# First FFN of a two-block transformer kernel: vectors loaded from ScalarE's queue, constants behind the weights, the context's second half turned ahead of the down products

## The reference, cut to what matters

```python
def swiglu(x, w_gate, w_up, w_down):
    return (jax.nn.silu(x @ w_gate) * (x @ w_up)) @ w_down
# first stage of first_block:  x = layer_norm(ALPHA * x + 0.5 * swiglu(x, gate, up, down), g, b)
```

## Time and profile before

| | us |
|---|---|
| median of 3 runs | 2466.32 (2464.76 to 2466.33) |
| profiled execution | 2465.18 |
| its span (first to last instruction) | 2462.6 |
| PE busy | 2277.5 (92% of the span) |
| DVE busy | 1439.2 (58%) |
| ACT busy | 1129.9 (46%) |
| mean granted TensorE clock | 0.964 of 2.4 GHz |
| DMA, mean over the span | 141 GB/s |

### The profile page before, as it was taken

The page is one execution under the profiler, slowest core; times in us unless marked ns, Lnnn a source line. Parts: engine busy times, 40 slices in busy tenths (PEclk is TensorE's granted clock), DMA queues, the critical chain, the costliest instruction groups (busy, mean ns, idle before and its releaser), DMA issues. The chain is left out here.

```text
span 2462.6 us, 37937 instructions
## 1 busy us (share of the span) xinstructions
PE 2277.5 (92%) x14504; PEld 1882.8 (76%) x14504; DVE 1439.2 (58%) x2366; ACT 1129.9 (46%) x1918; POOL 80.2 (3%) x117
## 2 busy tenths in 40 slices
PE   6999989999999989999769997889999989998998
PEld 6787967888888877877447886668888778876886
DVE  6565257667665347665554666364545554446886
ACT  3344254444443345444266665343434444445554
POOL 0000000000000000000001222000000000000000
PEclk9999999999999999999899999889999988998999
DMA  8786334875887414873112120144343353304662
GB/s 240 235 268 211 63 120 151 268 258 155 252 265 231 110 69 145 261 250 112 53 42 74 49 70 2 35 120 125 105 126 106 112 144 86 94 2 146 196 190 92
DMA packets 389938, 346.83 MB, mean 141 GB/s; under 512 B 24388, under 2 KB 353464, under 8 KB 389304
## 3 DMA queue, kind: packets, MB, share of 16 engines
q1 hardware_dynamic: 380600, 294.80, 40.6%
q10 hardware_dynamic: 9216, 50.34, 5.2%
HBM read 344.05 MB, written 1.05 MB: 140 GB/s over the span
## 5 line engine op out<-in xcount | busy, mean ns | idle before, releaser
L693 PE MATMUL ps<-x_hi_lo,gu_hi 128*128 128x512 f32 x1680 | 423.7, 394 | 1.9 <-DVE gu_sum L878 1.9
L693 PEld LDWEIGHTS ps<-x_hi_lo,gu_hi 128*128 128x128 f32 x1680 | 305.6, 188 | 80.9 <-issue 18.7
L878 DVE TENSOR_REDUCE gu_sum<-ps 128x256 f32<-128x512 f32 x220 | 150.6, 689 | 251.0 <-PE ps L695 248.8
L781 ACT ACTIVATE gu_hi<-w_gu 128x1024 fp32r<-128x1024 f32 x220 | 229.6, 1054 | 128.2 <-DVE gu_sum L878 52.8
L861 DVE TENSOR_TENSOR gu_lo<-w_gu,gu_hi 128x1024 fp32r<-128x1024 f32 x220 | 260.7, 1219 | 23.1 <-ACT gu_hi L781 22.9
L695 PEld LDWEIGHTS ps<-x_hi_lo,gu_lo 128*128 128x128 f32 x1680 | 228.8, 190 | 16.8
L695 PE MATMUL ps<-x_hi_lo,gu_lo 128*128 128x256 f32 x1680 | 233.8, 282 | 0.0
L722 PE MATMUL ps<-dn_hi,h_hi 128*128 128x512 f32 x440 | 174.2, 396 | 13.7 <-DVE h_lo L903 13.7
L722 PE MATMUL ps<-dn_lo,h_hi 128*128 128x512 f32 x440 | 173.2, 394 | 0.0
L722 PE MATMUL ps<-dn_hi,h_lo 128*128 128x512 f32 x440 | 171.9, 391 | 0.0
L797 ACT ACTIVATE silu<-gu_sum 128x256 f32<-128x256 f32 x88 | 36.7, 417 | 265.0 <-DVE gu_sum L878 264.4
(11 more groups left out here) (464 smaller groups left out, 4794.8 us busy)
## 6 DMA issues: line engine op xcount, KB each, us to landing
w_gu<-in_ffn_w_up SPq DMA_DIRECT2D x176, 512.0 KB, 6.3
w_dn<-in_ffn_w_down SPq DMA_DIRECT2D x132, 512.0 KB, 3.5
w_mod<-in_w_mod ACTq DMA_DIRECT2D x64, 768.0 KB, 7.0
w_gu<-in_ffn_w_gate SPq DMA_DIRECT2D x88, 512.0 KB, 5.1
odd_w<-in_odd_w_qkv SPq DMA_DIRECT2D x24, 512.0 KB, 5.2
w_gu<-in_ffn_w_down SPq DMA_DIRECT2D x11, 1024.0 KB, 4.9
hgrn_w<-in_even_w_in SPq DMA_DIRECT2D x20, 512.0 KB, 3.9
wo<-in_w_out SPq DMA_DIRECT2D x2, 4096.0 KB, 13.2
```

The source lines that it names most:

```text
L693: pe.matmul(gu(a), gu_hi[n][:, a, f, :], x_both[:, f, :, :], start=(f == 0), stop=False, skip_group_check=True)
L781: act.activation(gu_hi[n][:, a, :, :], wgu[n][:, a, :, :], ACT.Copy).then_inc(s["w_hi"], 1)
L878: dve.reduce_sum(c[n][:, a, :], gu(a).rearrange("p h t -> p t h"), AX.X).then_inc(s["c_ready"], 1)
```

## The change

The 15 vector loads leave SP's `load_rest` and become `load_vectors`, which ACT issues first of all, behind a one-column activation that reads a cleared cell. SP keeps constants and taps in `load_rest`. The context's two loads become `load_context`. The first pair of loads of the loop is written out for the first FFN: SP issues tile 2's gate and up part, its down part (when `dn_split` 1 has come), then the context, then tile 3; the loop starts one pair later. In step 3, `turn_rest` moves ahead of `down(2)` on TensorE, and `keep_rest` moves on DVE from the end of the step to right behind the reductions. Steps 1 and 2 keep the old order. Other FFNs of the program have no `Begin` and keep their code.

```diff
--- before.py
+++ after.py
@@ -478,6 +478,7 @@
         self.rows = ctx.enter_context(nc.sbuf_tensor("par_rows", [P, PAR_TILES, P], F32))
         self.x_rows = ctx.enter_context(nc.sbuf_tensor("x_rows", [P, TT, D], F32))
         self.causal = ctx.enter_context(nc.sbuf_tensor("causal", [P, P], F32))
+        self.warm = ctx.enter_context(nc.sbuf_tensor("warm", [P, 1], F32))
         self.consts = [(self.causal[:, :], w["c_causal"]), (k.cmp_mask[:, :, :], w["c_cmp"]),
                        (k.any_cmp[:, :], w["c_any"]), (k.unit[:, :], w["c_unit"]), (k.pick[:, :], w["c_stack"])]
 
@@ -487,18 +488,26 @@
             sp.dma_start(self.x_rows[:, tt, :], self.w["x"][0, tt * P:(tt + 1) * P, :]).then_inc(s["x_in"], 16)
         sp.dma_start(self.k.alpha[:, :], self.w["c_alpha"]).then_inc(s["alpha_in"], 16)
 
+    def load_vectors(self, act, s):
+        w, rows = self.w, self.rows
+        act.wait_ge(s["rows_zeroed"], 1)
+        act.activation(self.warm[96:P, :], rows[96:P, 2, 0:1], ACT.Copy)
+        for name, tile, r in self.VECTORS:
+            a = w[name]
+            src = a.rearrange("(r p) -> r p", p=P) if len(a.shape) == 1 else a.rearrange("l (r p) -> (l r) p", p=P)
+            act.dma_start(rows[r:r + src.shape[0], tile, :], src).then_inc(s["rows_in"], 16)
+
     def load_rest(self, sp, s):
         w, rows = self.w, self.rows
         for dst, src in self.consts:
             sp.dma_start(dst, src).then_inc(s["const_in"], 16)
         sp.wait_ge(s["rows_zeroed"], 1)
-        for name, tile, r in self.VECTORS:
-            a = w[name]
-            src = a.rearrange("(r p) -> r p", p=P) if len(a.shape) == 1 else a.rearrange("l (r p) -> (l r) p", p=P)
-            sp.dma_start(rows[r:r + src.shape[0], tile, :], src).then_inc(s["rows_in"], 16)
         taps = w["ffn_conv_w_2"].rearrange("l j (r p) -> (l j r) p", p=P)
         for n in range(CONV):
             sp.dma_start(rows[0:88, 2 + n, :], taps[88 * n:88 * n + 88, :]).then_inc(s["rows_in"], 16)
+
+    def load_context(self, sp, s):
+        w = self.w
         sp.wait_ge(s["x_turned"], FT // 2)
         for tt in range(TT):
             sp.dma_start(self.x_rows[:, tt, :], w["ctx_2"][0, tt * P:(tt + 1) * P, :]).then_inc(s["ctx_in"], 16)
@@ -670,9 +679,17 @@
                     else:
                         load_gu(n, n)
                         load_dn(n, n)
+                ahead_of_loop = 1 if begin else 0
                 if begin:
                     begin.load_rest(sp, s)
-                with sp.Fori(0, NF // 2 - 1) as j:
+                for n in range(2 * ahead_of_loop):
+                    sp.wait_ge(s["gu_split"], n + 1)
+                    load_gu(n + 2, n)
+                    sp.wait_ge(s["dn_split"], n + 1)
+                    load_dn(n + 2, n)
+                    if n == 0:
+                        begin.load_context(sp, s)
+                with sp.Fori(ahead_of_loop, NF // 2 - 1) as j:
                     for n in range(2):
                         sp.wait_ge(s["gu_split"], j * 2 + n + 1)
                         load_gu(j * 2 + (n + 2), n)
@@ -751,9 +768,11 @@
                         gate_up(t, n)
                     if mod and fixed == NF - 3:
                         mod_to_columns()
+                    if begin and fixed == 3:
+                        begin.turn_rest(pe, s, fixed)
                     if fixed is None or fixed >= 1:
                         down(t - 1, 1 - n, first=(fixed == 1 and not ln))
-                    if begin and fixed is not None:
+                    if begin and fixed is not None and fixed < 3:
                         begin.turn_rest(pe, s, fixed)
 
                 if begin:
@@ -774,6 +793,9 @@
 
             @block.scalar
             def _(act):
+                if begin:
+                    begin.load_vectors(act, s)
+
                 def hi_gu(t, n, a, fixed):
                     if a == 0:
 
@@ -878,6 +900,8 @@
                         dve.reduce_sum(c[n][:, a, :], gu(a).rearrange("p h t -> p t h"), AX.X).then_inc(s["c_ready"], 1)
                     if fixed == 0:
                         lo_dn(0, 5)
+                    if begin and fixed == 3:
+                        begin.keep_rest(dve, s, fixed)
                     if conv is not None:
                         dve.wait_ge(s["c_ready"], t * 2 + 2)
                         dve.wait_ge(s["mid_ready"], t * 2 + 2)
```

## The result

The changed kernel takes 2451.43 us (median of 4, 2450.14 to 2451.77) beside 2466.32 (median of 4): 14.9 us less, ratio of all runs 0.9936 with a 95% interval of 0.9921 to 0.9950. The predicted 2454.7 is 3.3 us above the measured median. That median lies at the lower end of the range of 2451.2 to 2461.2; by the ratio, 0.9936 times 2466.32 is 2450.5, just under it. The profiled execution took 2451.77, its span 2449.1, so between the two profiled executions the difference is 13.4 us, in span 13.5.

A forecast was written before the change was run, and what follows sets the result against it. TensorE bounds the kernel, with holes only before 64.8 us. Terms -12.1 first hole and clock, +0.2, +1.3, +0.1, +1.8, -2.8 second hole save 11.6 us: 2453.6, plus 1.14 to the median gives 2454.7 (2451.2 to 2461.2).

The forecast's parts named there:

- the two new waits of the sum: TensorE's predicted new waits: +1.3 us ahead of `down(1)` and +1.8 us ahead of the second context transposes.
- What bounds the kernel, and that savings before 64.8 us carry over: TensorE never idles in FFN steps from 64.8 to 204 us, so time saved earlier is saved for the whole program.
- Start, +0.2 (0 to 0.8): At the start, ACT's 15 issues fit its slack until 12.3 us; vector transfers delay the tokens by 0.2 us.
- First hole, -11.9: Ahead of `down(0)`: tile 2 issued earlier removes 9.9 us of hole and 2.2 of slow clock; `gate_up(2)` starts at 30.0.
- New wait ahead of `down(1)`, +1.3: Tile 3 lands at 33.0, `h_lo` ends at 36.9, TensorE is ready at 35.7: +1.3 us (0 to 3).
- Parameter copies, +0.1: After `down(1)`, DVE makes the parameter copies at about 39.8; no more than 0.1 us of wait.
- Second context transposes, +1.8: Behind `gate_up(3)`, TensorE waits for DVE's late context copies, done at 48.2: +1.8 us (0 to 2.5).
- Second hole, -2.8: Ahead of `mod_turn`: with the second half turned early, the 2.78 us wait for the context copies is gone.
- One generator for both queues: At the start, ACT's issues stall with SP's: 4.0 to 7.7 us behind 12.3, 2458.7 to 2462.4 us; chance 0.12.
- ACT's issues at 1.71 us each: Rival: every ACT issue costs SP's worst vector, ending at 27.9, before the first `gu_hi`; 2470.3 us, slower; chance 0.04.
- The waits only move: Both landings and DVE late by their bounds: 2459.6 us, chance 0.10; tile 2 later still, 2464 to 2466, chance 0.06.
- No new waits: Tile 3 lands by 31.7 and DVE is on time: 3.2 us more saved, 2451.5 us; chance 0.10.

The follow-up runs named there:

- the queues alone: The changed kernel with the context's second half turned where it was before, on both TensorE and DVE: 2459.65 us, ratio 0.9974.
- DVE's order alone: The changed kernel with TensorE's second context transposes back behind `down(2)`, DVE's copies staying right behind step 3's reductions: 2454.80 us, ratio 0.9946.
- The kernel with copies sooner: The changed kernel with constants and taps behind tile 2's loads and, in step 2, DVE's first-half context copies before `dn_lo` of tile 3: 2452.61 us, ratio 0.9936.
- the kernel with the context first: The changed kernel with the context's loads ahead of tile 2's in SP's queue, vectors still by ACT: 2453.76 us, ratio 0.9954.

## Why the prediction came out as it did

Two steps failed: the two new waits of the sum (3.1 us together, 0.8 measured, made up in part by a first hole 1.2 us worse than predicted), and the step that took every later stage over at its old time. Each moved the result by about 1 us.

**What bounds the kernel, and that savings before 64.8 us carry over: right** to 0.01 us up to the end of the FFN (166.90 and 166.91). **That nothing else would differ later failed**, as the prediction put it: "what is saved before 64.8 us is saved for the whole program". The later stages have short idle stretches in which the granted clock falls in one kernel and not in the other, and the distance moves both ways: from 12.56 to 13.49 at the end of this FFN, and between 11.8 and 15.4 behind it. In the two profiles of the changed kernel the whole span is 0.9 and 1.3 us further ahead than `gate_up(4)` is. The profile of the queues alone lost 3.7 us in this way (5.11 at `gate_up(4)`, 1.4 in span); at 2464.22 it is 4.6 above that kernel's median. The range had no term for it. From `gate_up(4)` to the end, TensorE in the kernel before, the changed one, the queues alone and DVE's order alone:

```profile
64.76:2462.60 2397.84, 2233.03 (x14241) 0.96 0.45 138
52.20:2449.10 2396.90, 2234.69 (x14241) 0.96 0.45 139
59.65:2461.20 2401.55, 2238.75 (x14241) 0.96 0.45 138
52.00:2453.60 2401.60, 2237.83 (x14241) 0.96 0.45 138
```

The same 14241 matmuls take 2233.0 to 2238.8 us, and that is the clock. But in the changed kernel they take 1.7 us more than in the kernel before, and the rest is 0.9 shorter all the same, as TensorE is idle for 2.6 us less. So what the later stages gave is not the clock alone; what the idle time hangs on wasn't followed. Over the thirteen profiles here this rest takes 2396.1 to 2401.6 us, and the 0.9 lies inside that spread.

**Start, +0.2 (0 to 0.8): within its bounds, reason wrong.** The tokens were not late (6.51 and 6.52). ACT was done at 8.72, earlier than the 9.3, as the first issue began at 1.63 already, ahead of `warm`. The slack was real: doubling the issues kept ACT to 15.16, 2.9 beyond the 12.3, and the first pass started 2.8 later. What I missed is that ACT's issues lengthen SP's: tile 1 came 0.8 to 1.5 later, and in the first profile this made `gate_up(1)` 0.47 late. Over all profiles little of it reaches TensorE: `gate_up(1)` started at 20.36 to 21.10 in the nine with ACT's 15 issues, at 20.50 to 20.66 in the three without.

**First hole, -11.9: direction and cause right, 1.2 us too large.** It measured 41.88 - 31.13 = 10.75. SP came to tile 2 at 17.25 instead of the 15.6 worked out, which is its later release from the first weights; hence 0.77 (1.44 when repeated) of a wait that I had at 0 with a bound of 2.5. The rest is the start, 0.47 late instead of 0.2, and 0.1 in `down(0)`. The sum's 1.0 to 1.7 us from the last byte to the semaphore stand in no row and no run shows them; from issue to landing the load took 6.4 us, as assumed. The slow clock behind the hole, 2.2, was right: 5.62 became 3.51.

**New wait ahead of `down(1)`, +1.3: this term failed, it was 0.** Tile 3 landed at 32.60 (31.92 when repeated), not 33.0, and `h_lo` was done at 36.4; TensorE, late from tile 2, asked at 36.8. The two landings are coupled: what tile 2 loses hides the wait for tile 3. I had carried a tile 2 without any wait and a wait for tile 3 into one sum. The kernel in which SP loads the vectors behind tile 2 shows the other side: no wait at `down(0)`, 3.1 at `down(1)`.

**Parameter copies, +0.1: nothing. Second context transposes, +1.8: mechanism right, mis-sized,** 0.80 and 0.00. DVE's chain hangs on tile 3's landing, which was 0.4 us sooner than worked out; its steps from there to the copies were 0.9 shorter in sum, so the copies were done at 46.92, not 48.2.

**Second hole, -2.8: right against the kernel before, but not what the edit is worth.** I took it for independent of the queues. It isn't: with them alone the hole was 7.0 us and cost the clock too, in a profile with tile 5 late; the two parts save 5.1 and 2.8 alone and 12.6 together. The expectation of 55.5 to 56 for the queues alone, worked out without a late tile 5, would make the early turn worth 3.3 to 3.8 us (an estimate; no profile of that order had tile 5 on time). The half of the edit which counts for most is DVE's copies ahead of the wait for tile 5; I had argued it as a matter of TensorE's order.

In sum the stage gave 12.56 (13.28) where 11.6 were predicted: 1.0 to 1.7 more, from waits that did not come, less what SP lost at the start. The profiled pair has 0.9 on top from the later stages, and the medians another 1.5: the prediction added 1.14 because the profiled execution of the kernel before was that much under its median, while the changed kernel's is 0.34 above its own. Whether these 1.5 are chance can't be said.

**Rivals.** One generator for both queues: refuted in its strong form, that ACT stalls with SP, by ACT's issues of 0.5 us beside SP's of 3.17; SP's issues do stretch, by 0.5 to 1.6 us in sum. The Trainium skill's section "Queues, rings and completion order" of "DMA: Bandwidth & Descriptors" doesn't speak against this rival: it gives SP and ACT a ring each on the same engines, but no descriptor generator of their own. That SP's issues stretch agrees with something shared; what it is, no run shows. The rule of the same page that a second issuer saves only issue time ("Issuing engines are not separate DMA queues") agrees as well: the issue time that ACT took over was worth 3.6 us of stage time through SP's queue. ACT's issues at 1.71 us each: none took more than 0.66. The waits only move: of its 4.9 us, 0.8 came, at tile 2. No new waits: nearly what happened in the stage. That its 2451.5 is the measured median is luck, as it has 14.8 us saved in the stage, which gave 12.6 to 13.3.

**Open.** The kernel with DVE's order alone has the changed kernel's first FFN (52.00 beside 52.20) and a median of 2454.80. The kernel with copies sooner, run in the same group, has 2452.61, the changed kernel in the others 2451.43 and 2452.33; but the intervals of the ratios overlap (0.9931 to 0.9961 and 0.9921 to 0.9950), so a difference of 2 to 3 us is not sure. Its profiled execution is the slowest of its four. In it the distance falls from 13.2 to 7.6 us between 236 and 980 us of the kernel before, and from `gate_up(4)` to the end it takes 4.7 us more than the changed kernel's first profile, 3.1 of it in matmuls at the lower clock. Why they fell that way wasn't settled. The other way round, the kernel with the context first made up for what it lost in the stage:

```profile
53.12:2449.20 2396.08, 2231.21 (x14241) 0.97 0.45 139
```

## What to carry over

In a stage where one engine is otherwise always busy, follow each load that comes next once a hole is removed, together with its consumer's new start; the waits for two coupled landings don't add. An engine that works in order should do what another one waits for ahead of its own next wait on a transfer: the copy's place on DVE, more than the transposes' on TensorE, decided up to 7 us here, with the awaited transfer late. And when a change shifts the rest of a program, leave room on either side for what later stages make of it (here the rest took 2396.1 to 2401.6 us with no edit in it), and read the stage, not only the total.

## What was not expected of the hardware

ACT began to issue at 1.63, before its own activation at 2.05 that stands ahead in the program, and beside its table load. Issues by ACT beside stalled issues by SP went through in 0.5 us each, but SP's second down load then took 3.44 to 3.98 us to issue instead of 3.07, and 3.33 with hardly any bytes in ACT's loads. The same load of tile 5's up part, beside the same 1.5 MB of `w_mod`, landed 6.3 us after its issue in one profile and 12.2 in another. Behind a hole of 3.1 us stood half clock over the next 5.25 us in one kernel (0.84 granted in the 3.18 us around the hole), while one of 2.78 left the clock at full, as did one of 2.99 in the kernel with the context first; and 2.02 us without matmuls were followed by half clock in the kernel before and by full clock in the changed one.
